# Modulation weights unsplit on four quarters of the array, with buffers of their own, and the input norm on token rows

## The reference, cut to what matters

```python
def rms_norm(x, g):
    y = xf * lax.rsqrt(jnp.mean(xf * xf, axis=-1, keepdims=True) + RMS_EPS)
    return (y * g).astype(x.dtype)

sh1, sc1, ga1, sh2, sc2, ga2 = split(silu(c)     @ w_mod + b_mod)   # w_mod: 2048 x 12288
csh1, csc1, ...              = split(silu(c_ctx) @ w_mod + b_mod)
px = (rms_norm(x,   norm_mix) * (1 + sc1)  + sh1)  @ w_in
pc = (rms_norm(ctx, norm_mix) * (1 + csc1) + csh1) @ w_in
...
y = (y - mean(y)) * rsqrt(var(y) + GN_EPS) * ln_w + ln_b            # heads of 64
y = y + sum(r * (kf + kb) * r_k) * v
...
on = (o - mean(o)) * rsqrt(var(o) + EPS)                            # retention, heads of 128
```

## Time and profile before

| | |
|---|---|
| median of 3 runs | 3165.48 us |
| profiled execution, its own time | 3176.06 us |
| its span | 3174.3 us |
| PE busy, DVE busy, ACT busy | 97%, 66%, 50% of the span |
| `mod`, to the first main matmul | 11.5 to 149.7 us |
| `in_kv` | 149.7 to 439.8 us |
| `in_rest` | 518 to 650 us |
| scan of the first block | 667 to about 1150 us |
| `in_2_heads`, with retention | to about 2317 us |

### The profile page before, as it was taken

The page is one execution under the profiler, slowest core; times in us unless marked ns, Lnnn a source line. Parts: engine busy times, 40 slices in busy tenths (PEclk is TensorE's granted clock), DMA queues, the critical chain, the costliest instruction groups (busy, mean ns, idle before and its releaser), DMA issues.

```text
span 3174.3 us, 62635 instructions
## 1 busy us (share of the span) xinstructions
PE 3072.8 (97%) x26939; PEld 2651.8 (84%) x26939; DVE 2100.7 (66%) x2893; ACT 1571.4 (50%) x2161; POOL 245.6 (8%) x307
## 2 busy tenths in 40 slices
PE   6799999999999998999999999999999999999998
PEld 4578888888888887888888888888878888888887
DVE  5776656767787867555555556679986666665554
ACT  5555545565665644444444434456644444444333
POOL 1000000023332310000000000012200000000000
PEclk9899999999999999999999999999999999999999
DMA  9667766820000034666666565665545555665564
GB/s 335 201 212 245 244 223 212 253 82 8 11 9 8 8 104 152 199 186 186 186 186 187 178 196 179 218 177 160 156 154 184 186 186 186 186 186 187 185 188 143
DMA packets 549246, 529.56 MB, mean 167 GB/s; under 512 B 16916, under 2 KB 545706, under 8 KB 548074
## 3 DMA queue, kind: packets, MB, share of 16 engines
q1 hardware_dynamic: 546074, 516.08, 52.1%
q0 software_dynamic: 2832, 9.45, 0.9%
q10 hardware_dynamic: 64, 0.02, 0.0%
HBM read 521.28 MB, written 4.19 MB: 166 GB/s over the span
## 4 chain that ended last, share of the span: by engine, by line
PE 86%; DVE 9%; ACT 2%; DMA 2%; issue 1%; POOL 0%; DVEq 0%; ACTq 0%; POOLq 0%
PE ps L2003 39%; PE ps L2004 19%; PE ps L2134 10%; DVE lo L1216 3%; PE ps L2013 2%; PE ps L2042 2%; PE ps L2014 2%; PE ps L2015 2%; PE ps L2043 2%; PE ps L2396 1%; PE ps L2157 1%; PE ps L2144 1%; PE ps L2142 1%; ACT hi L800 1%; PE ps L2397 1%
## 5 line engine op out<-in xcount | busy, mean ns | idle before, releaser
L1216 DVE TENSOR_TENSOR lo<-raw,hi 128x1024 fp32r<-128x1024 f32 x936 | 1137.6, 1235 | 654.0 <-ACT hi L800 651.1
L800 ACT ACTIVATE hi<-raw 128x1024 fp32r<-128x1024 f32 x936 | 972.5, 1055 | 829.3 <-PE ps L2004 594.1
L2003 PE MATMUL ps<-mov,hi 128*128 128x512 f32 x3680 | 1303.3, 399 | 6.0 <-DVE mov L1278 4.8
L2004 PE MATMUL ps<-mov,lo 128*128 128x256 f32 x3680 | 1032.7, 281 | 0.0
L2003 PEld LDWEIGHTS ps<-mov,hi 128*128 128x128 f32 x3680 | 691.9, 188 | 180.8 <-issue 6.3
L2004 PEld LDWEIGHTS ps<-mov,lo 128*128 128x128 f32 x3680 | 695.4, 189 | 0.1
L2003 PE MATMUL ps<-hid,hi 128*128 128x512 f32 x704 | 248.8, 399 | 0.0
L2042 PE MATMUL ps<-hi,c 128*32 128x256 f32 x768 | 190.6, 288 | 40.2 <-DVE lo L1216 40.0
L820 ACT ACTIVATE tmp<-ps 128x512 f32<-128x512 f32 x157 | 93.8, 597 | 269.8 <-PE ps L2004 263.1
L2004 PE MATMUL ps<-hid,lo 128*128 128x256 f32 x704 | 197.7, 281 | 0.0
L2043 PE MATMUL ps<-lo,c 128*32 128x256 f32 x768 | 187.5, 284 | 0.0
(11 more groups left out here) (373 smaller groups left out, 4148.5 us busy)
## 6 DMA issues: line engine op xcount, KB each, us to landing
raw<-in_w_in SPq DMA_DIRECT2D x184, 512.0 KB, 4.6
raw<-in_w_mod SPq DMA_DIRECT2D x160, 512.0 KB, 4.9
raw<-in_w_gate SPq DMA_DIRECT2D x88, 512.0 KB, 4.5
raw<-in_w_up SPq DMA_DIRECT2D x88, 512.0 KB, 4.4
raw<-in_w_down SPq DMA_DIRECT2D x88, 512.0 KB, 4.6
raw<-in_w_ffn_gate SPq DMA_DIRECT2D x88, 512.0 KB, 4.6
raw<-in_w_ffn_up SPq DMA_DIRECT2D x88, 512.0 KB, 4.5
raw<-in_w_ffn_down SPq DMA_DIRECT2D x88, 512.0 KB, 4.3
```

The source lines that it names most:

```text
L800: act.activation(hi[:, s, :, :], src, ACT.Copy).then_inc(hi_ready, 1)
L1216: dve.tensor_tensor(lo[:, s, :, :], raw_at(ph, i, j)[0], hi[:, s, :, :].bitcast(F32), ALU.subtract)\
L2003: pe.matmul(ps[:, b, :], hi[:, s, kk, w], moving(k, None), start=first, stop=False)
L2004: mm = pe.matmul(ps[:, b, 0:T], lo[:, s, kk, w], moving(k, 0), start=False, stop=last)
```

## The change

- Chunks of `w_mod` are no longer split. `mod_rows` issues one float32 matmul for each of the 4 k-blocks, `c4` as float32 against the raw chunk, each to its own 32 rows of the bank and so to its own quarter (128 x 32) of the array. The four quarters accumulate apart, and the column matmul, now over 128 partitions, adds them up through `sel`.
- The side chunks have 4 raw buffers of their own, `spare_hi` and `spare_lo`, which are the places 2 and 3 of the `hi` and `lo` rings; the main chunks of `in_kv` and `in_rest` are split into places 0 and 1 alone. A load of a side chunk waits for PE, no longer for DVE. `all_chunks` works out each chunk's buffers and waits.
- Side chunks stand in threes ahead of every main chunk of `in_kv`, and singly ahead of each main chunk of `in_rest`.
- The input norm sums squares by token rows: 8 ACT squares of 128 x 1024 with an accumulator, the root on 128 x 4, and `diag`, four diagonal 128 x 128 matrices of the roots. The transpose and the multiplication by the root are one float32 matmul by `diag`, and ACT multiplies by the gain while it copies out of PSUM. x is transposed once more for the residual.
- The mean of the group norm is taken off v by a matrix `less_mean64` in the matmul that transposes v; L2184 and L1558 go. POOL's copy `rv` goes.

The diff, cut to its core:

```diff
@@ class Phase
             for c in self.rows_order:
-                self.order.append((False, p, c))
                 per = SIDES.get(name, 0) // pairs
-                if c < per:
-                    self.order += [(True, per * p + c, e) for e in range(n)]
+                self.order += [(True, per * p + t // n, t % n) for t in range(per * c, per * c + per)] + [(False, p, c)]
...
-    lookahead = lambda ph: 2 if ph.name in EARLY else 3
+    lookahead = lambda ph: 4 if ph.name == "in_kv" else 2 if ph.name in EARLY else 3
...
-                if stage == "c":
-                    gnp.wait(dve, "mean", b)
-                    gnd.done(dve.scalar_tensor_tensor(out=y, in0=ps[:, bank, 0:T], scalar=-1.0 / HEAD, in1=y, op0=ALU.mult, op1=ALU.add), "c")
...
+    spare = [at("spare_hi", 24 * KIB, [P, 2, CK, CN]), at("spare_lo", 40 * KIB, [P, 2, CK, CN])]
+    def all_chunks():
+        ...
+                if ph.name == "mod":
+                    buffer = g % (2 * RING)
+                else:
+                    buffer = RING + sides % RING if whole else mains % RING
+                    sides, mains = sides + whole, mains + (not whole)
+        ...
+                if buffer in in_buffer:
+                    last, load = in_buffer[buffer]
+                    raw_free = (split_free, last + 1 + SPLIT_CREDIT) if out[last].whole else (lo_ready, out[last].split)
...
             def retention(h):
-                retg.done(pool.tensor_copy(rv[:, :], one(p2, h + RV)), "v")
                 retg.done(pool.tensor_tensor(rqc[:, :, :], qk_of(h), both(rcos), ALU.mult), "qc")
...
+                for k in scaled_at_pair(p):
+                    if k == 0:
+                        act.wait_ge(gain_ready, 2)
+                    act.wait_ge(normed_turned, k + 1)
+                    for n in (2 * k, 2 * k + 1):
+                        q, _, dest = first_operand(n)
+                        act.activation(dest, ps[:, TURN[k % 4], (1 - q) * T:(2 - q) * T], ACT.Copy, scale=gain[:, q, k:k + 1]).then_inc(nt_ready, 1)
+            def squares(i, j):
+                if j in SQUARE_AT:
+                    ...
+                    act.activation(junk[:, :], (crow, xrow)[col // 2][:, col % 2, half * D // 2:(half + 1) * D // 2], ACT.Square,
+                                   accum_out=row_sum[:, half, col:col + 1]).then_inc(row_squared, 1)
...
+                dve.tensor_tensor(diag[:, :, :], ident.rearrange("p (a n) -> p a n", a=1).broadcast_to([P, 4, P]),
+                                  y.rearrange("p (a n) -> p a n", n=1).broadcast_to([P, 4, P]), ALU.mult).then_inc(diag_ready, 1)
...
-                        pe.wait_ge(lo_ready, ph.chunk(i, j) + (1 + RING))
+                        if ph.whole(j):
+                            src, arrived, loads = raw_at(ph, i, j)
+                            pe.wait_ge(arrived, loads * 16)
+                        else:
+                            pe.wait_ge(lo_ready, chunks[ph.chunk(i, j)].split)
...
-            def mod_rows(b, s, kk, k, first, last):
-
-                pe.matmul(ps[0:32, b, 0:CN], c4[:, k, :], hi[:, s, kk, :], start=first, stop=False)
-                return pe.matmul(ps[0:32, b, 0:CN], c4[:, k, :], lo[:, s, kk, :], start=False, stop=last)
+            def mod_rows(b, src, c):
+
+                for kk in range(CK):
+                    cols = slice(32 * kk, 32 * kk + 32)
+                    mm = pe.matmul(ps[cols, b, 0:CN], c4[:, c * CK + kk, :].bitcast(F32), src[:, kk, :], start=(c == 0), stop=(c == KB // CK - 1))
+                return mm
...
+                for k in normed_at(p):
+                    if k == 0:
+                        pe.wait_ge(diag_ready, 1)
+                    if k >= 4:
+                        pe.wait_ge(nt_ready, 2 * (k - 3))
+                    for n in range(4):
+                        mm = pe.matmul(ps[:, TURN[k % 4], n * P:(n + 1) * P], (crow, xrow)[n // 2][:, n % 2, k * P:(k + 1) * P], diag[:, n, :],
+                                       start=True, stop=True)
+                    mm.then_inc(normed_turned, 1)
...
-                    retg.wait(pe, "v", h)
+                    pe.wait_ge(bank_free, trip_out(h))
                     for n in range(2):
-                        mm = pe.matmul(ps[:, 7, n * P:(n + 1) * P], rv[:, n * P:(n + 1) * P], less_mean, start=True, stop=True)
+                        mm = pe.matmul(ps[:, 7, n * P:(n + 1) * P], one(p2, h + RV)[:, n * P:(n + 1) * P], less_mean, start=True, stop=True)
```

More of the change, by code:

```diff
@@ L8 @@
+import dataclasses
 from contextlib import ExitStack
@@ L105, in completed, with whole @@
         return (side, p) if c == self.last_rows(side) else None
+    def whole(self, j):
+        return self.name == "mod" or (j < self.chunks and self.order[j][0])
     def last_rows(self, side):
@@ L194, in constants @@
     sel = np.zeros((P, P), f)
-    sel[0, 0] = sel[1, 0] = sel[2, 1] = sel[3, 1] = 1
+    for first in range(0, P, 32):
+        sel[first:first + 2, 0] = 1
+        sel[first + 2:first + 4, 1] = 1
     n = np.arange(HEAD)
@@ L602, in load_vectors @@
+    chunks = all_chunks()
+    def raw_at(ph, i, j):
+        c = chunks[ph.chunk(i, j)]
+        n = c.buffer - RING
+        if n < 0:
+            tile = raw[:, c.buffer, :, :]
+        elif ph.chunk(i, j) < PH["in_kv"].g0:
+            tile = raw_more[:, n, :, :]
+        else:
+            tile = spare[n // 2][:, n % 2, :, :]
+        return tile, raw_in[c.buffer], c.load
     def load_vectors(eng, which):
@@ L790, in _ @@
             chain = Chain(act, a_chain)
+            split_done = set()
             def split(ph, i, j):
-                if isinstance(i, int) and ph.chunk(i, j) >= TOTAL:
+                g = ph.chunk(i, j)
+                if g >= TOTAL or chunks[g].whole or g in split_done:
                     return
-                s = ph.slot(j)
+                split_done.add(g)
+                s = chunks[g].half
                 src, arrived, loads = raw_at(ph, i, j)
                 act.wait_ge(arrived, loads * 16)
-                act.wait_ge(split_free, ph.chunk(i, j) + 1)
+                if chunks[g].half_free:
+                    act.wait_ge(split_free, chunks[g].half_free)
                 act.activation(hi[:, s, :, :], src, ACT.Copy).then_inc(hi_ready, 1)
@@ L850, in _ @@
                 act.activation(c4[:, :, 2 * q:2 * q + 1], csil[:, q, :], ACT.Copy).then_inc(chi_ready, 1)
-            for j in range(2):
-                split(PH["mod"], 0, j)
             def turn(i, p):
@@ L910, in shift_r @@
                                    scale=vcol("shift_rkv", n + 3 * RB)).then_inc(shift_ready, 1)
+            split(PH["in_kv"], 0, 3)
             gemm(PH["in_kv"], shift_both, first_groups)
@@ L1211, in split @@
             def split(ph, i, j):
-                if isinstance(i, int) and ph.chunk(i, j) >= TOTAL:
+                g = ph.chunk(i, j)
+                if g >= TOTAL or chunks[g].whole or g in split_done:
                     return
-                s = ph.slot(j)
-                dve.wait_ge(hi_ready, ph.chunk(i, j) + 1)
+                split_done.add(g)
+                s = chunks[g].half
+                dve.wait_ge(hi_ready, chunks[g].split)
                 dve.tensor_tensor(lo[:, s, :, :], raw_at(ph, i, j)[0], hi[:, s, :, :].bitcast(F32), ALU.subtract)\
@@ L1634, in unit @@
                         y_rows(YROWS[l - 3])
-                    if norm is not None and l == 2:
-                        group_norm(norm, "c")
                     if q and b and l == 5:
@@ L2182, in group_norm @@
             def group_norm(b, stage, bank=1, gate_bank=7):
-                if stage == 2:
-                    gnp.done(pe.matmul(ps[:, bank, 0:T], blk64, ymix[:, ds(b, 1), :], start=True, stop=True), "mean")
                 if stage == 4:
@@ L2315, in last_norm @@
             def last_norm(i, j):
-                if i == 0 and j == 0:
-                    for e in range(2):
-                        scan_y[e].wait(pe, "y", RB - 1)
-                    group_norm(RB - 1, 2, bank=5)
                 if i == 0 and j == 1:
```

206 lines of the change are left out of this document (119 added, 87 removed).

## The result

The changed kernel took **3124.24 us** (median of 4 runs, 3121.24 to 3126.05) against 3158.78 us for the kernel before (4 runs, 3145.86 to 3172.03): ratio 0.9878, 95% interval 0.9846 to 0.991. Measured once more, beside other kernels: 3111.98 us (6 runs) against 3162.34 (11 runs), ratio 0.9829, interval 0.9789 to 0.9869. So it is faster by 1.2 to 1.7%, where 3.0% was forecast (3165.5 to 3070). The range held the time, but the forecast gain of 95.5 us was 2.8 times the 34.5 us of the first comparison and 1.9 times the 50.4 us of the second.

The account below looks back on a forecast made before the run. PE was taken to bound the kernel, busy 97% of the span, with DMA's pace deciding in mod. Gains of 30 + 40 + 15.6 + 7.9 + 3.5 = 97 us off 3165.5 gave 3070 us, range 3035 to 3130.

Parts of the forecast that it names:

- The quarters: Side chunks' four float32 matmuls on PE run at once in four array quarters: 0.46 us a chunk instead of 1.72.
- The rule of the Trainium skill: Weight loads overlap matmuls only across different row groups; its rival: 1.32 us per side chunk, 3178 us, chance 0.07.
- mod: Modulation phase: DMA at 350 GB/s sets the end; first main matmul at 119.5 instead of 149.7 us, gain 30.
- in_kv: Stage of 290.1 us: PE's shorter stream plus 16 us of stalls sum to 250, gain 40 us.
- a rival with a chance of 0.12: in_kv: main loads issued behind side loads land late; a round takes 8.8 instead of 7.8 us, 3100 us total; chance 0.12.
- in_rest: Stage of 132 us: PE's shorter stream takes 110 us, 6.5 us of idle time stay; gain 15.6 us.
- Retention: Retention heads: PE's waits for POOL's copy rv go, at the last head only POOL's 1.33 us; gain 7.9 us.
- mean: Group norm in the scan: mean matmuls on PE and subtractions on DVE go; gain 3.5 us, at most 6.7.

Follow-up runs that it names:

- main_first: Changed kernel with SP issuing each in_kv main chunk's load ahead of its three side chunks' loads; 3082.89 us, ratio 0.9749 to the kernel before.
- both: Changed kernel with in_kv main chunks' loads issued first and column matmuls behind the next main chunk; 3061.62 us, ratio 0.97 to the kernel before.
- after_again: The changed kernel without further edits, measured once more in more rounds; 3111.98 us.
- filler: Changed kernel with four useless float32 matmuls on PE ahead of each in_kv wait for a side chunk's row copy; 3131.71 us, ratio 0.9895 to before.
- cols_late: Changed kernel with in_kv's column matmuls issued behind the next main chunk, loads' order untouched; 3097.27 us, ratio 0.9817 to the kernel before.
- early_split: Kernel of both, with ACT and DVE splitting in_kv's first main chunk ahead of the first eight shifts; 3059.53 us, ratio 0.9678 to the kernel before.
- both_again: The kernel of both measured once more, in more rounds beside the changed kernel; 3059.7 us, ratio 0.9684 to the kernel before.

## Why the prediction was wrong

**The quarters: right.** 0.43 to 0.45 us a chunk against 0.46, shown by the records and by one and two quarters beside them. The weight loads stay hidden, 16 of them in two chunks' 0.9 us (ns min/median/max):

```profile
L2126 PEld LDWEIGHTS ps<-spare_hi,c x16: 106/110/110, 201.2 to 201.7; 128*32 128x32 f32 x16
```

The rule of the Trainium skill that I had weighed ("TensorE: Matmul & The Clock Gate", Part 3, "What overlaps and what doesn't") would show them, since the row groups are the same; here the measurement decides against it.

**`mod`: right in its mechanism, 3 to 6 us too good.** DMA's pace sets the end, at 344 GB/s where I had taken 350. The first main matmul came at 125.3 instead of 119.5. The last modulation matmul started at 113.8, some 4 us behind the forecast, and from there to the first main matmul were 11.5 us, where the forecast had 6.8 and 3 for the clock. The loads' order has at most a small part in it: with the main load first it came at 122.9 (main_first), 123.8 and 122.9 (both), but in three other profiles with the changed kernel's own order of loads, after_again, filler and cols_late, at 124.3, 122.3 and 122.4. I had put the three side chunks "beneath" the shift, while they are three more transfers behind the last of `mod` (early_split).

**`in_kv`: this step failed.** The sum had 0.5 us of stalls in each of 32 rounds, 16 us. The stage took 297.7 us where PE's own stream was priced at 234: 64 us, four times that, or 2 us a round. I had named each piece: a side chunk's load that holds back a main one, the row copy behind a split, the column one side chunk behind. But I priced them as independent tenths and gave the first to a rival with a chance of 0.12. They are one chain: SP blocked, main chunk late, split late, copy behind it late, PE waiting at the column. It closes on itself: SP's second side load of the round shown above hangs from 203.43 until PE has used a side buffer at 208.33, and PE's wait at the column holds up the next. The rival's place was right, and its price, 8.8 us a round, was near the measured one (four rounds in 36.1 us). The price was so in part by luck: how 8.8 follows from its 7.9 us of landing and 2.3 us of splits is not shown. Its argument against itself was wrong (a ring of four side buffers with one over did not cover a queue that issues in order). Of the 57 us that the two edits gave back, 37 are idle time of PE (41.1 to 4.0) and 20 its busy time, some 14 of these the granted clock by the filler run, which neither the forecast nor the rival had: the prediction allowed for a lower clock in `mod` alone. The other 6 of its busy time are not explained. PE's stream itself was priced 2.5 us too low (236.6 in both_again): the 5.24 us of the earlier trace rows for a main chunk's 23 steps is the shorter of two values in the kernel before, 5.35 the other, and 5.36 is the usual one now.

**`in_rest`: 11.7 instead of 15.6**, with 0.3 us a round for entering and leaving the float32 group that was not in the price. PE is busy 118.6 us where 110 was priced, and idle 4.1 where 6.5 was left. The gain was also counted from a stretch that ended too early: PE's last matmul of the phase before starts at 653.6, not by 650, which hides some 3.5 us of the shortfall.

**Retention 9.4 (7.9), mean 3.0 (3.5): right** within what a profile can tell. Of the 9.4, the waits gave 8.0 and the clock behind the last of them the rest.

With the two edits that take the stall away, the stages' gains sum to 97.3 us, where the forecast had 97. That the two sums agree so closely is luck: `in_kv` gave 9.5 us more than its term, since 4.0 us of stalls came where 16 were priced, and `mod`, `in_rest` and `in_lora` with `in_r` gave 9.9 less. For the kernel as it was changed, the forecast was wrong.

## What to carry to other kernels

When a change makes the consumer of one kind of load faster, walk through the engine's program that issues all loads: where one program issues them in order, the least urgent load, blocked on its buffer, holds the most urgent one (50.6 us of `in_kv` here). Issue the load first whose data has the longest way to go (here a transfer, two splits and 24 matmuls), and price a chain of small waits as a loop, by its period in the timeline, not as a sum of tenths. Where a change opens idle stretches on TensorE, look for the granted clock behind them and price it too.

## What the runs showed of the hardware

**Two paces of the same stream.** In the long PE-bound stretches of untouched code, with no idle time and a granted clock of 1.00, one kernel's PE issues more matmuls in the same 400 us than another's. Changed kernel first, then main_first, both from 1300 to 1700 us:

```profile
1300.00:1700.00 400.00, 400.00 (x2309) 349.80 (x2308) 223.53 (x217) 189.43 (x217) 0.00 (x0) 1.00 0.61 190
```

```profile
1300.00:1700.00 400.00, 400.00 (x2266) 346.79 (x2266) 218.61 (x213) 185.01 (x210) 0.00 (x0) 1.00 0.60 187
```

2309 against 2266 records, 1.9%; 700 matmuls take some 121.3 or 123.7 us in such stretches of all profiles. A phase keeps its pace to its end: from norm to norm, the first of two long phases took 750 or 764 us and the second 728 or 742, and all four combinations occur. 29 runs of the kernel before on one chip lay at 3145 to 3150 (14 runs), 3158 to 3163 (8) and 3172 to 3178 us (7). In the first comparison the profile of before had the slower pace in both phases and that of the changed kernel in one, which makes the 14 us between their spans that no edit accounts for. What sets the pace is open; nothing here was tried on it. For an edit of a few us, a stage's own length in the profile tells more than the median.

**Float32 matmuls in column quarters run side by side, nearly without loss**: 1.74, 0.88 and 0.45 us a chunk on one, two and four quarters that share all rows.
